# The experts' queries and first layer from unnormed x, with the norm's factor put onto their tiles

## The reference

```python
def rms_norm(x, g):
    y = xf * lax.rsqrt(jnp.mean(xf * xf, axis=-1, keepdims=True) + EPS)
    return (y * g.astype(F32)).astype(x.dtype)

h = h + mem_cross_attention(hn, mem_n, w_q_mem[i], w_kv_mem[i], w_o_mem[i])
hn = rms_norm(h, norm_ffn_g[i])
h = h + peer(hn, peer_w_q[i], peer_keys[i], peer_u[i], peer_v[i])

def peer(h, w_q, sub_keys, u_tab, v_tab):      # cut
    q = (h @ w_q)                               # 8 heads x 128
    s = jnp.einsum("blhsk,hsnk->blhsn", q, sub_keys)
    s1, i1 = lax.top_k(s[..., 0, :], 16); s2, i2 = lax.top_k(s[..., 1, :], 16)
    ...                                         # top 16 of the 256 pair sums, softmax g
    act = jax.nn.gelu(h @ u_tab[idx]);  out = (g * act) @ v_tab[idx]
```

## Time and profile before

| | |
|---|---|
| median of 3 runs | 4038.54 us (4037.6 to 4041.47) |
| the profiled execution's own time | 4032.62 us |
| its span (first to last instruction) | 4030.8 us |
| PE busy | 3793.3 us, 94% |
| DVE busy | 2761.9 us, 69% |
| ACT busy | 2101.8 us, 52% |
| mean granted clock of PE | 0.978 of full speed |

### The profile page before, as it was taken

The page is one execution under the profiler, slowest core; times in us unless marked ns, Lnnn a source line. Parts: engine busy times, 40 slices in busy tenths (PEclk is TensorE's granted clock), DMA queues, the critical chain, the costliest instruction groups (busy, mean ns, idle before and its releaser), DMA issues. The chain is left out here.

```text
span 4030.8 us, 65797 instructions
## 1 busy us (share of the span) xinstructions
PE 3793.3 (94%) x22128; PEld 3140.5 (78%) x22128; DVE 2761.9 (69%) x5248; ACT 2101.8 (52%) x3953; POOL 259.6 (6%) x279
## 2 busy tenths in 40 slices
PE   7899988989999999895999989999889999999998
PEld 2577764868888887754888778888768888888887
DVE  3564456778886677796865575788786666666667
ACT  1453424456655565485454445555685555555554
POOL 4000000100000012061000000000000000000000
PEclk9999999999999999998999999999999999999999
DMA  9775543756665555522555355666327765656654
GB/s 352 268 259 183 189 152 155 284 172 212 211 213 188 188 189 183 159 79 84 168 182 184 123 172 162 215 209 210 124 75 222 223 203 189 189 188 189 190 184 162
DMA packets 204828, 753.89 MB, mean 187 GB/s; under 512 B 23859, under 2 KB 23892, under 8 KB 202708
## 3 DMA queue, kind: packets, MB, share of 16 engines
q1 hardware_dynamic: 181492, 667.00, 51.3%
q0 software_dynamic: 21696, 79.01, 5.4%
q10 hardware_dynamic: 1440, 5.24, 0.3%
HBM read 725.99 MB, written 25.17 MB: 186 GB/s over the span
## 5 line engine op out<-in xcount | busy, mean ns | idle before, releaser
L211 DVE TENSOR_TENSOR weights_lo<-ring,weights_hi 128x512 fp32r<-128x512 f32 x2240 | 1531.6, 698 | 921.8 <-ACT weights_hi L204 911.7
L204 ACT ACTIVATE weights_hi<-ring 128x512 fp32r<-128x512 f32 x2240 | 1397.4, 630 | 1337.5 <-PE ps L1176 1274.7
L1176 PE MATMUL ps<-expert_parts,weights_hi 128*128 128x512 f32 x4224 | 1458.0, 394 | 12.2 <-DVE expert_parts L1129 7.0
L1176 PE MATMUL ps<-expert_parts,weights_lo 128*128 128x256 f32 x4224 | 1140.7, 280 | 0.0
L1176 PEld LDWEIGHTS ps<-expert_parts,weights_hi 128*128 128x128 f32 x4224 | 778.2, 188 | 174.3 <-issue 14.9
L1176 PEld LDWEIGHTS ps<-expert_parts,weights_lo 128*128 128x128 f32 x4224 | 796.1, 188 | 21.5
L1176 PE MATMUL ps<-in_parts,weights_hi 128*128 128x512 f32 x1408 | 493.5, 397 | 12.4 <-DVE weights_lo L211 11.3
L1176 PE MATMUL ps<-in_parts,weights_lo 128*128 128x256 f32 x1408 | 381.1, 281 | 0.0
L1176 PE MATMUL ps<-hidden,weights_hi 128*128 128x512 f32 x1024 | 351.5, 392 | 0.6 <-DVE weights_lo L211 0.6
L1176 PEld LDWEIGHTS ps<-in_parts,weights_hi 128*128 128x128 f32 x1408 | 260.9, 189 | 71.0 <-issue 11.5
L1176 PE MATMUL ps<-hidden,weights_lo 128*128 128x256 f32 x1024 | 275.9, 280 | 0.0
(11 more groups left out here) (520 smaller groups left out, 4668.6 us busy)
## 6 DMA issues: line engine op xcount, KB each, us to landing
ring<-in_w_mlp SPq DMA_DIRECT2D x256, 512.0 KB, 3.7
ring<-in_w_u SPq DMA_DIRECT2D x256, 512.0 KB, 4.2
ring<-in_w_v_tab SPq DMA_DIRECT2D x256, 512.0 KB, 4.2
ring<-in_w_mix SPq DMA_DIRECT2D x88, 512.0 KB, 4.7
ada_ring<-in_w_ada SPq DMA_DIRECT2D x72, 512.0 KB, 6.8
ada_ring<-in_w_ada POOLq DMA_DIRECT2D x64, 512.0 KB, 6.5
ring<-in_w_out SPq DMA_DIRECT2D x64, 512.0 KB, 3.9
ring<-in_w_in SPq DMA_DIRECT2D x48, 512.0 KB, 4.1
```

The costliest lines, as they stand in the source:

```text
L204: act.activation(core.hi[:, g % SLOTS], core.ring[:, slot, at:at + QUARTER], ACT.Copy).then_inc(core.rounded, 1)
L211: dve.tensor_tensor(core.lo[:, g % SLOTS], core.ring[:, slot, at:at + QUARTER], core.hi[:, g % SLOTS].bitcast(F32), ALU.subtract).then_inc ...
L1176: mm = pe.matmul(out, part[:, g % SLOTS, k, :], moving, start=at == 0 and part is core.hi, stop=last and part is core.hi)
```

## The change

The input of the experts is no longer normed before it is split. While mem_out runs, each tile of x is multiplied by the norm's gain and rounded on ACT (`GrownSplit.round`) and subtracted on DVE (`SplitBeside.split`), one tile behind, into mem_parts; the last two splits stand behind the last tile. mem_parts, the tensor that holds the parts of the normed memory until values are made, is kept for it in place of expert_parts. mem_out and peer_q are now written out. At the start of peer_q PE sums the squares and ACT takes the root as before; DVE's reciprocal moves behind the addition of peer_q's tile 0, and the factor by token (in the first 256 columns of params) is multiplied onto each of the 8 tiles of queries, the 72 of experts_first and the 56 of up, between the addition and what follows.

```diff
+class GrownSplit(SplitBeside):
+    def __init__(self, core, gain, parts):
+        self.core, self.gains, self.parts = core, (gain,), parts
+        self.done = {n: core.spare.pop() for n in ("grown", "rounded")}
+    def issue(self, pool):
+        pass
+    def round(self, act, n):
+        self.done["grown"].wait(act, n + 1)
+        act.activation(self.parts[:, n, 0, :], self.core.x[:, n, :], ACT.Identity, bias=self.core.small[:, ZERO_COL:ZERO_COL + 1],
+                       scale=self.gains[0][:, n:n + 1]).then_inc(self.done["rounded"].sem, 1)
+
+class LateNorm:
...
+    def tensor(self, pe):
+        pe.matmul(self.total, self.core.ones[:], self.squares, start=True, stop=True).then_inc(self.summed.sem, 1)
+    def scalar(self, act):
+        self.summed.wait(act, 1)
+        act.activation(self.factor, self.total, ACT.Sqrt, bias=self.core.small[:, EPS_COL:EPS_COL + 1],
+                       scale=1.0 / D).then_inc(self.rooted.sem, 1)
+    def inverse(self, dve, n):
+        self.rooted.wait(dve, 1)
+        self.core.dve.step(dve, dve.reciprocal(self.factor, self.factor))
...
                         if layer.scale is not None:
                             core.dve.step(dve, ins)
-                            if n == 0 and layer is layers[0]:
+                            if late is not None and n == 0 and layer is layers[0]:
                                 late.inverse(dve, 0)
                             ins = dve.tensor_tensor(slot, slot, layer.scale, ALU.mult)
...
-def onto_stream(core, last=True):
+def onto_stream(core, last=True, grown=None):
...
             add_squares(core, dve, n, slots[0])
+        if grown is not None:
+            dve.sem_inc(grown, 1)
...
-        linear_stage(core, "mem_out", [Layer("w_o", KD, [parts], finish=onto_stream(core), squares=True, steps=3)], ("w_peer_q", 0))
+        split = GrownSplit(core, core.prm["norm_ffn"], mem_parts)
+        linear_stage(core, "mem_out", [Layer("w_o", KD, [parts], finish=onto_stream(core, grown=split.done["grown"].sem),
+                                             squares=True, steps=3)], ("w_peer_q", 0), beside=split)
+    parts = mem_parts
+    scale = core.params[:, 0:T]
...
-            linear_stage(core, "peer_q", [Layer("w_peer_q", PEER_HEADS, [parts], into=lambda n: q[:, n, :],
-                                                source=gates[:, 0:KD, :],
-                                                norm=Norm(core.x, core.prm["norm_ffn"], squares=core.squares))],
-                         ("w_u", 0), loads=[(keys, "peer_keys")])
+            linear_stage(core, "peer_q", [Layer("w_peer_q", PEER_HEADS, [parts], into=lambda n: q[:, n, :], scale=scale)],
+                         ("w_u", 0), loads=[(keys, "peer_keys")], beside=Beside(), late=LateNorm(core, core.squares, scale))
...
-                Layer("w_u", EARLY_TILES, [parts], shape=lambda act, n, slots: gelu(act, choice.act_slot(act, n), slots)),
+                Layer("w_u", EARLY_TILES, [parts], scale=scale, shape=lambda act, n, slots: gelu(act, choice.act_slot(act, n), slots)),
...
-            up = Layer("w_u", KEYS - EARLY_TILES, [parts], finish=gate_experts, first=2 * EARLY_TILES,
+            up = Layer("w_u", KEYS - EARLY_TILES, [parts], scale=scale, finish=gate_experts, first=2 * EARLY_TILES,
```

More of the change, by code:

```diff
@@ L614, in last_vector, with __init__, ready, over @@
         self.split(dve, KD - 1)
+class GrownSplit(SplitBeside):
[9 more added lines that the diff above has]
+class LateNorm:
+    def __init__(self, core, squares, factor):
+        self.core, self.squares, self.factor = core, squares, factor
+        self.total = core.ps[:, NORM_BANK, 0:T]
+        _, self.summed, self.rooted, _ = core.norm_signals
+    def ready(self, dve):
+        pass
+    def tensor(self, pe):
[7 more added lines that the diff above has]
+        self.core.dve.step(dve, dve.reciprocal(self.factor, self.factor))
+    def over(self):
+        self.summed.base += 1
+        self.rooted.base += 1
 class LateNorms:
@@ L3045, in after_tile, with second_block @@
             dve.scalar_tensor_tensor(x, x, self.core.prm["final1"][:, k:k + 1], self.first_rstd, ALU.mult, ALU.mult)
-def second_block(core, out, in2, in2_space):
+def second_block(core, out, in2, in2_space, kept):
     nc = core.nc
@@ L3079, in second_block @@
         y = proj[:, 2 * HT:, :]
-        mem_parts = sb("mem_parts", [P, KD, 2, T], F32R)
+        mem_parts = kept.enter_context(nc.sbuf_tensor("mem_parts", [P, KD, 2, T], F32R, side="right"))
         with ExitStack() as out2:
@@ L3104, in second_block @@
         attention_stage(core, q, k, v, parts, h)
-        linear_stage(core, "mem_out", [Layer("w_o", KD, [parts], finish=onto_stream(core), squares=True, steps=3)], ("w_peer_q", 0))
-    with nc.sbuf_tensor("expert_parts", [P, KD, 2, T], F32R) as parts, nc.sbuf_tensor("gates", [P, KEYS, T], F32) as gates:
+        split = GrownSplit(core, core.prm["norm_ffn"], mem_parts)
[3 more added lines that the diff above has]
+    scale = core.params[:, 0:T]
+    with nc.sbuf_tensor("gates", [P, KEYS, T], F32) as gates:
         saved = nc.dram_tensor("saved_acts", (EARLY_TILES // 4, P, 4, T), F32, kind="Internal").ap()
@@ L3175, in two_block_kernel @@
         mlp_block(core, in2)
-        second_block(core, out, in2, in2_space)
+        with ExitStack() as kept:
+            second_block(core, out, in2, in2_space, kept)
 def shape_constants():
```

## The result

The changed kernel takes 4059.57 us (median of 6 runs, 4057.16 to 4065.17), the kernel before 4038.07 us beside it (6 runs, 4034.5 to 4041.47). The ratio is 1.0054, 95% interval [1.0044, 1.0065]: 21.5 us slower. The profiled execution took 4058.23 us, its span 4056.4 us, with a mean granted clock of 0.979. I had forecast 4051.2: slower by 12.7 us, with a range to 4059.5. The direction was right and the size was not; the median lies just above the range.

What follows compares the result with a forecast made beforehand. PE was taken to set the pace nearly everywhere, 5.55 us a tile, except for a hole after mem_out. Terms -6.6, +0.45 and +18.8 summed to +12.7 us on 4038.54, giving 4051.2, range 4044 to 4059.5.

Steps and rivals of the forecast that it cites:

- The hole: PE's 12.2 us gap between mem_out's last and peer_q's first product shrinks: -6.6 us, with 0.3 given back in the clock ramp.
- mem_out: One added rounding on ACT and split on DVE per tile stay hidden behind PE's 5.55 us a tile: cost 0.
- peer_q's end: The multiplication behind peer_q's last tile stands between the last product and the stage's end: +0.45 us, once.
- experts_first: DVE's added 0.45 us a tile puts it over PE's pace in 59 tiles: net +18.8 us.
- the need that I had worked out: In experts_first, DVE's busy time plus 1.00 idle and 0.45 a tile: 24.2 us over PE's pace in 59 tiles.
- the lead and the records: Taken off in experts_first: about 1 us for splits' lead, 1.2 us for busy records outlasting the next start.
- up: DVE's 3.86 us a tile plus 0.45 and waits for ACT stays under 5.55 in this experts stage: cost 0.
- Rival 3: All 59 experts_first tiles pay in full, on top of the old losses: +20.4 us, 4059; chance 5%.
- Rivals 1 and 2: In experts_first, searches absorb it, only 19 wide-operation tiles pay: 4041, 8%; or the splits' lead hides all: 4032.4, 4%.
- Rival 4: PE's clock falls in experts_first because PE stops in most tiles: +140 us on half of 59 tiles, 4190; chance 2%.
- Rival 5: The up stage falls behind too, 56 tiles at 0.45: 25 us more, 4076; chance 2%.
- What would show it: Hole about 6 us, ACT's waits 0.45 longer, experts_first additions 5.9 to 6.1 apart, weights_lo waits some 24, none in mem_out or up.

Runs made afterwards that it cites:

- the 64 bytes: Changed kernel with 64 bytes left free at the end of SBUF, so mem_parts starts at byte 196512 instead of 196576: 4057.79 us, ratio 1.005 to before.
- the place alone: Kernel before with only expert_parts moved to the right end of SBUF, byte 196576 instead of 58144: 4049.96 us against 4038.38, ratio 1.0033.
- the gelu a tile later: Changed kernel with ACT's gelu of each experts_first tile put behind the copy of the next tile: 4037.52 us, ratio 1.0001 to before.
- the gelu later: Kernel before with ACT's gelu in experts_first a tile later and nothing else: 4034.05 us, ratio 0.999.
- the pads: Kernel before with the gelu a tile later and pads putting large inputs at 32 modulo 256: 4027.76 us, ratio 0.997.
- the map: Kernel before with two added stages timing product pairs at 64 input starts, 32 bytes apart: the pair times repeat every 256 bytes within 0.0009 us.
- the two places kernels: Kernel before with pads of 32 to 1376 bytes moving mem_parts, att_parts and expert_parts, in two versions: 4068.08 and 4067.15 us, one run each.

## Why the prediction was right and wrong

- **The hole, -6.6 (-5.7 to -7.1).** Right in its mechanism, and too small. The first product starts 6.65 us earlier, set against mem_out's last addition (6.3 forecast): the last split ends 1.12 us behind its rounding's start where 1.25 was taken, the sums' product starts 0.31 behind that end where 0.54 was, and the first real product 0.55 behind it where 0.6 was. The rest, 1.06 us and not 0.3, came back in the ramp: between the two additions the granted clock was 0.86 on the mean instead of 0.66. In all it is 7.7, outside the range that I gave; this term was mis-sized by 1.1.
- **mem_out, 0.** Right: 83.35 us from first to last addition in both.
- **peer_q's end, +0.45.** Not to be seen: peer_q itself grew by 0.35 us through the place. From its last addition to experts_first's first it took 16.05 before and 14.91 after, and with it the granted clock rose from 0.68 to 0.77 on the mean; what the one multiplication costs there can't be told apart from that (below).
- **experts_first, +18.8.** The mechanism was right: DVE's program in order, its idle microsecond, 0.45 on top. The size near PE's old pace is 20.1 (420.56 us with the 64 bytes, against 400.42), at the new pace 17.9 of 20.8. The stretches lost 5.0, 1.4, 5.9 and 7.8 us, 20.1 in all where 18.8 was forecast. Against the need that I had worked out, the first came out 1.8 us lower (5.80 us a tile instead of 5.89, since DVE's busy time grew by 0.32 a tile there and not 0.45) and the last 1.2 higher (6.16 instead of 6.08). The whole is 0.8 below the need, where I had taken off 2.2 for the lead and the records; so errors of both signs cancel in part.
- **up, 0, and with it all that follows: the step that failed.** The prediction asked only whether DVE stays "under 5.55" us a tile and took PE's pace as given, here and in mem_out, peer_q and experts_first. It is not given: it hangs on where the input starts, and the change moved the input. The place of the input was no term of the sum. This cost 0.7 us in mem_k, 0.35 in peer_q, 2.9 in experts_first and 8.6 in the experts, 12.6 us in all. The run with the place alone cost 11.6 by the medians, with mem_k's input left where it was. That mem_parts takes the place of expert_parts stood in my account of the change, and the profile of before had the price: the tiles of in2 and of the MLP's first layer took 5.607 us at the same address. I read the pace of the experts' stages only. A further 0.95 is the factor at the end of up, where I had looked at busy shares and not at what is queued behind the last tile.
- **The rivals.** Rival 3 named 4059, the time that came, but not for its reason: DVE's part was 17.9 to 20.1 us and not 26.6, and the time came from the place. The rule of the Trainium skill that it would have followed from (VectorE: DVE Perf Modes, The DRAIN you can't avoid) I had read too widely: the same section says that a next operation that is not held starts earlier. The trace agrees with that after the change too, four splits of 0.69 us still take 2.50. Rivals 1 and 2 fall with 5.80 us a tile in the searches. Rival 4 falls with a granted clock of 1.00 in four of the five stretches and 0.98 in the one where PE was idle for 6 of 98.5 us; what the Trainium skill says of frequent small idle times (TensorE: Matmul & The Clock Gate, A second HAM failure mode: psum-queue depth-cycling) did not show here. Rival 5, that up falls behind, fell as well: its loss was no wait.
- **What would show it.** "PE's waits for weights_lo from 5 to some 24 us": they went to 13.3, for what seems to be the same reason. Sums of waits are too low a measure here; distances between equal instructions are not. ACT's waits for experts_first's sums grew by 1.3 us a tile and not 0.45 (from 89.4 us in 59 waits to 162.1 in 58, in the stretches of the earlier trace rows). The additions were 5.80 to 6.16 us apart, as forecast, and no new wait of PE over 1 us appeared in another stage: the signs that I had named could not have shown the place.

Summed by its parts: -7.7 and -1.1 at the two stage starts, +17.9 for the factor in experts_first, +12.6 for the place, +0.95 at up's end, 22.7 us; the medians differ by 21.5.

## What to carry to other kernels

When an edit changes which tensor an inner loop reads, compare the pace of that loop by the start of equal instructions, in stages that already read from the new address; the 5.55 us that I called PE's own were those of one start modulo 256. Before work is put onto an engine that runs in order, ask which idle time in its program is only an order of another engine's program: moving one instruction there (the gelu a tile later) took back the whole cost of the 0.45 us a tile. And where a change does two things, move each alone before judging the idea: here the idea is worth 6 to 8 us, and the moved input and the factor in experts_first cost 30.

## What the runs showed of the hardware

- The time of products with 512 and 256 moving columns (fp32r operands) depends on the start of the moving operand modulo 256 bytes: a pair takes 0.3467 to 0.3533 us, 1.9% between the best start (32 or 160) and the worst (128). It shows with PE alone. Why, no run here tells.
- Between peer_q's last addition and experts_first's first, the granted clock set the time. The windows of before, of the changed kernel and of the kernel with the place alone:

```profile
2462.70:2478.80 16.10, 15.35 (x76) 13.93 (x77) 3.15 (x7) 5.23 (x8) 0.00 (x0) 0.68 0.29 96
```

```profile
2459.30:2474.30 15.00, 13.76 (x76) 12.38 (x77) 3.62 (x8) 5.23 (x8) 0.00 (x0) 0.77 0.29 106
```

```profile
2469.40:2480.80 11.40, 10.64 (x76) 9.62 (x77) 3.18 (x7) 5.25 (x8) 0.00 (x0) 1.00 0.41 133
```

In the first and the last, PE was idle for the same 2.04 us and then did the same 76 products, and yet the granted clock was 0.68 on the mean in one and 1.00 in the other: 16.05 and 11.32 us from addition to addition. PE's busy time times the granted clock is 10.4, 10.6 and 10.6 us in the three windows. It looks like more than scatter of single executions: three further kernels that have expert_parts at 58144 and no factor took 15.99 to 16.01 us at 0.68 (the gelu later, with and without the pads, and the map), and four further ones with the change 14.87 to 14.93 us at 0.77. But the changed kernel with the 64 bytes alone took 16.49 at 0.69, and the two places kernels 14.5 at 0.76. What decides how long the clock stays low there, no run tells. Comparing stretches between stage starts keeps it apart from the rest.
